# A linear recurrence computed ahead of 14 projection tiles, with another form of its factor, over eight banks

## The chip, the core and the metric

One core of a Trainium2 chip runs the whole program in a single launch. The metric is the device time of one execution in microseconds (us); all arithmetic is in float32.

## What is computed

The reference is a transformer layer followed by a second layer of another kind, for one sequence of 256 positions of width 1024. The first layer is a feed-forward block, a mixer and a second feed-forward block. The change lies in the mixer. Cut to what matters:

```python
proj = u @ w_in[l]                                   # 8704 columns
q, k, v, xr, yr, gl = jnp.split(proj, splits, axis=-1)
...                                                  # attention -> attn_d
xc = conv(xr) + conv_b                               # causal, width 4, per channel
gate_x = sigmoid(einsum(xc, w_x) + b_x)
gate_a = sigmoid(einsum(xc, w_a) + b_a)
log_a = -8.0 * gate_a * softplus(-a_param)
a = exp(log_a)
b = sqrt(-expm1(2.0 * log_a)) * (gate_x * xc)
h[t] = a[t] * h[t-1] + b[t]                          # over the 256 positions
rec_d = (h * gelu(yr)) @ w_rec_branch[l]
gates = sigmoid(gl)                                  # two sets of 1024
merged = gates[0] * attn_d + gates[1] * rec_d
h_out = h_in + rms_norm(merged @ w_out[l], mix_norm_post[l])
```

The second layer adds modulation from a condition vector, a grid shift, a bidirectional recurrent mixer with a Fourier part, and a feed-forward of 32 experts of which each position uses 4.

## The kernel before, in words

Activations of the mixer stand with channels on the 128 partitions and the 256 positions along the free dimension; a tile is 128 channels by 256 positions and is one accumulation in one of PSUM's eight banks (`ps[:, bank, 0:S]`). Weights come through a ring of eight slots of 128x3072 floats in SBUF. SP sends one load after the other in a fixed order (`send`, L389); load n waits until slot n-8 has been used (`w_used`). `N_WIN`, `N_LRU`, `N_ATT`, `N_REC`, `N_OUT` are the places in that order: 23 slots of `w_in` (three tiles each, the last two), two of the recurrence gates, two of the attention branch, three of the recurrence branch, three of the output projection. Then come 22 slots of the second feed-forward, with 16 of the modulation in between.

Each engine's program is written out by hand, and engines meet by semaphores; `up(name)` counts an event, `at(name, n)` awaits its n-th, `now(name)` the last one so far. Several events share a semaphore (`SHARED`, L190), so their order there is that of the engine's program.

After q, k, v and the attention, the mixer's rest runs as follows.

- TensorE (`rec_pe`, L722): 32 tiles of eight matmuls each over four banks (`proj_pe`, L520, matmul L529): 8 tiles of xr, 8 of yr, 16 of the gates gl. A tile waits until the one four before it has been read. Then 16 tiles of the recurrence gates with two matmuls each over eight banks (L746), the attention branch (8 tiles of four matmuls, L529), the recurrence branch (8 tiles of eight, L529), and the output projection (`out_pe`, L773, matmul L782), which waits until all eight merged tiles are there. From the fifth tile on, the attention branch waits until VectorE has merged the tile four before it.
- ScalarE (`rec_act`, L879): gelu on the yr tiles (L886), sigmoid on the gl tiles (L888), sigmoid on the recurrence gates (L892), eight tanh of -log_a (L897), one exp of log_a over all 128x2048 (L899), one square root over the same size (L902). A change of function table is an instruction of its own, ACT_TABLE_LOAD. Then the norm behind the output projection: two sums of squares (L414) and a small square root (L417).
- VectorE (`rec_dve`, L791): the convolution (five operations a tile, L824 to L832), gate_x times xc (L838), log_a (L843), then the factor under the root from t = tanh(-log_a), since 1 - a^2 = 2t / (1 + t): t + 1 (L847), reciprocal (L849), times t (L851), each over 128x2048. Then the attention branch's eight merges (L855), the product under the recurrence (L858), eight scans (L861), times gelu(yr) (L863), and the recurrence branch's merges (L867, L869).

Much later, the expert stage begins with the experts 0 and 1; `bias_up_pe` (L2125) adds their biases by a matmul whose weights are columns of the computed order `perm`. Its call is in `moe_pe`.

Of the kernel before, what the change touches and what calls it, by code (L numbers as in the profile page):

```python
# [14 lines left out]
P = 128  # L15
D = 1024
KD = D // P
S = 256
# [33 lines left out]
N_LRU = N_WIN + 23  # L52
N_ATT = N_LRU + 2
# [8 lines left out]
assert N_MOE % RING == 0  # L62

# [33 lines left out]
def shape_constants():  # L97
# [42 lines left out]
    cols["expert"] = np.tile(e, 4)[:, None]  # L140
    cols["room"] = np.tile(BS - np.array(CAPACITY)[None], (P, 1))
# [36 lines left out]
for _name, _rows in COLUMN_ROWS:  # L178
    if _n // P != (_n + _rows - 1) // P:
# [11 lines left out]
    "pe_1": (("cols_tp", 1), ("ext_mm", 12), ("qk", 16), ("v", 4), ("att_scores", 8), ("rec", 21), ("lru", 14),  # L191
# [3 lines left out]
    "act_1": (("sp_exp", 1), ("qk_out0", 12), ("v_out0", 4), ("att_exp", 8), ("gate_out", 24), ("lru_gate", 16),  # L195
              ("lru_tanh", 8), ("lru_sqrt", 1), ("cs", 2), ("p_read", 20), ("lora", 2), ("xcs", 8), ("spec", 4),
              ("fno", 4), ("catT", 2), ("rowb", 4), ("ek", 2)),
    "dve_1": (("cols", 2), ("ext", 12), ("qk_out1", 12), ("v_out1", 4), ("att_scored", 8), ("decay8", 1),
              ("xr_out", 8), ("lru_gx", 8), ("lru_ratio", 1), ("att_merged", 8), ("recT", 1), ("rec_merged", 8),
# [15 lines left out]
def build(nc, x, out):  # L215

    with ExitStack() as ctx:
# [144 lines left out]
        for i in range(23):  # L362
            wide(N_WIN + i, x["w_in"][0], 384 * i, min(384, 8704 - 384 * i), KD)
# [156 lines left out]
        def proj_pe(pe, tag, n, tiles, i0, freed, kt=KD, src=None, width=S, lo=0):  # L520


            landed(pe, n)
            src = uT if src is None else src
            w = slot(n)[:, 0:kt * tiles * P].rearrange("p (k n) -> p k n", k=kt)
            for c in range(tiles):
                freed(i0 + c)
                for k in range(kt):
                    ins = pe.matmul(ps[:, (i0 + c) % 4, 0:width], w[:, k, c * P:(c + 1) * P], src[:, k, lo:lo + width],  # L529
                                        start=(k == 0), stop=(k == kt - 1))  # L530
                ins.then_inc(*up("w_used" if c == tiles - 1 else tag))
# [18 lines left out]
        REC = tiles_of(N_WIN + 12, (3,) * 10 + (2,))  # L550
# [171 lines left out]
        def rec_pe(pe):  # L722
# [8 lines left out]
            for s in range(11):  # L731
                proj_pe(pe, "rec", N_WIN + 12 + s, 3 if s < 10 else 2, 3 * s, freed)

            pe.wait_ge(*at("xc", LH))
            for gi in range(2):
                n = N_LRU + gi
                landed(pe, n)
                w = slot(n)[:, 0:2048].rearrange("p (q k n) -> p q k n", q=4, k=2)
                for o in range(LH):
                    i = gi * LH + o  # L740
                    if i < 4:
                        pe.wait_ge(*at("gate_out", 24 - 3 + i))
                    elif i >= 8:
                        pe.wait_ge(*at("lru_gate", i - 7))
                    for k in range(2):
                        ins = pe.matmul(ps[:, i % 8, 0:S], w[:, o // 2, k, (o % 2) * P:(o % 2 + 1) * P], xc[:, o // 2 * 2 + k, :],  # L746
                                            start=(k == 0), stop=(k == 1))
                    ins.then_inc(*up("w_used" if o == LH - 1 else "lru"))

            i = 0  # L750
            for n, tiles in ((N_ATT, 6), (N_ATT + 1, 2)):
                def freed(i):
                    if i < 4:
                        pe.wait_ge(*at("lru_gate", 8 + i + 1))
                    else:
                        pe.wait_ge(*at("att_merged", i - 3))
                proj_pe(pe, "attb", n, tiles, i, freed, kt=4, src=attnT)
# [3 lines left out]
            for n, tiles in ((N_REC, 3), (N_REC + 1, 3), (N_REC + 2, 2)):  # L761
# [5 lines left out]
                proj_pe(pe, "recb", n, tiles, i, freed, src=lb)  # L767
                i += tiles

            pe.wait_ge(*at("rec_merged", LH))  # L770
            out_pe(pe, N_OUT, merged)

        def out_pe(pe, n0, src):  # L773

            for k in range(KD):
                n = n0 + k // 3
                if k % 3 == 0:
# [13 lines left out]
        def rec_dve(d):  # L791
# [72 lines left out]
            d.wait_ge(*now("recT"))  # L864
            for t in RECB:
                tile_done(d, "recb", t)
                d.tensor_tensor(gates[:, 8 + t[1], :], ps[:, t[1] % 4, 0:S], gates[:, 8 + t[1], :], ALU.mult).then_inc(*up("dve_own"))  # L867
# [11 lines left out]
        def rec_act(a):  # L879
# [9 lines left out]
            for t in LRU_G:  # L889
                tile_done(a, "lru", t)  # L890
                dst = lb if t[1] < LH else la
                a.activation(dst[:, t[1] % LH, :], ps[:, t[1] % 8, 0:S], ACT.Sigmoid,  # L892
# [1285 lines left out]
        def moe_pe(pe, turns):  # L2178
# [8 lines left out]
            def first(s):  # L2187
# [6 lines left out]
                bias_up_pe(pe, [perm[:, r:r + 1] for r in BLOCKS[s]])  # L2194
# [320 lines left out]
```

## Time and profile before

| what | value |
|---|---|
| median of 3 runs | 2480.01 us (2478.4 to 2480.95) |
| profiled execution, own time | 2474.24 us |
| its span | 2472.4 us |
| granted TensorE clock, mean | 0.957 |
| TensorE busy | 2228.3 us (90%) |
| VectorE busy | 763.5 us (31%) |
| ScalarE busy | 305.7 us (12%) |
| HBM traffic | 234 GB/s over the span |

The span runs from the first to the last instruction that the profiler saw; the own time is that of the same execution from outside. Starts are counted from the span's beginning. PE is TensorE's matmuls, PEld its weight loads, DVE VectorE, ACT ScalarE, POOL GpSimd, SP the engine that issues the weight loads. A float32 matmul of the program appears as two records. The granted clock is a share of 2.4 GHz.

### The profile page before, as it was taken

The page shows a single profiled execution, that of the slowest core. Times are in us where ns is not written, and L with a number is a line of the kernel's source. Part 1 is how long each engine was busy: PE and PEld are TensorE (multiplying, and loading weights), DVE is VectorE, ACT ScalarE, POOL GpSimd, SP SyncE. Part 2 cuts the span into 40 slices and gives each one's busy share as a digit, 9 for nine tenths or more (in the row PEclk, how much of TensorE's full clock was granted, in tenths as well). Part 3 has the DMA queues.
Part 4 walks back from the last instruction along what each step waited for, and adds up shares of the span by engine and source line. Part 5 has one row for each costly group of instructions (what it writes and reads, how often), then busy time and mean ns, then how long its engine had stood idle before and what let it go on. Part 6 is the DMA issues. An engine that isn't in the chain of part 4 may idle for free.

```text
span 2472.4 us, 34348 instructions
## 1 busy us (share of the span) xinstructions
PE 2228.3 (90%) x15028; PEld 1372.9 (56%) x15029; DVE 763.5 (31%) x1257; ACT 305.7 (12%) x563; POOL 102.3 (4%) x117
## 2 busy tenths in 40 slices
PE   7999798996799994989998759999999999999995
PEld 5667685885477763467777634444344344334431
DVE  1000102405265407346778451121121121211123
ACT  1000101012100000243433200000000000000000
POOL 0000000000100000211221100000000000000000
PEclk9999999997999996999999969999999999999998
DMA  9555443242668960000000347999999999999995
GB/s 315 175 161 172 136 152 102 94 136 94 199 218 280 284 194 15 1 3 3 3 3 3 134 182 311 414 419 417 417 416 416 417 414 416 416 416 416 414 417 203
DMA packets 232599, 581.07 MB, mean 235 GB/s; under 512 B 10341, under 2 KB 154497, under 8 KB 199553
## 3 DMA queue, kind: packets, MB, share of 16 engines
q1 hardware_dynamic: 227472, 562.07, 60.0%
q0 software_dynamic: 4560, 14.83, 1.7%
q8 instruction: 120, 1.97, 0.3%
q10 hardware_dynamic: 416, 1.94, 0.2%
q14 instruction: 31, 0.25, 0.0%
HBM read 575.40 MB, written 3.41 MB: 234 GB/s over the span
## 4 chain that ended last, share of the span: by engine, by line
PE 79%; DVE 9%; DMA 4%; SPq 3%; ACT 2%; issue 1%; POOL 0%; DVEq 0%; ACTq 0%; POOLq 0%
PE ps L2138 18%; PE ps L461 13%; PE ps L529 9%; PE ps L2150 7%; PE ps L470 6%; PE ps L1015 4%; DMA ring<-in_w 4%; SPq L2064 3%; PE ps L2162 3%; PE ps L782 2%; PE ps L2117 2%; PE ps L613 2%; PE ps L1356 2%; PE ps L1376 1%; PE ps L1373 1%
## 5 line engine op out<-in xcount | busy, mean ns | idle before, releaser
L2138 PE MATMUL ps<-ring,arena 128*64 128x512 f32 (+1 forms) x2048 | 502.7, 595 | 11.7 <-DMA ring<-in_w 11.7
L2138 PEld LDWEIGHTS ps<-ring,arena 128*64 128x64 f32 (+1 forms) x2048 | 178.1, 144 | 335.1 <-issue 335.0
L461 PE MATMUL ps<-arena,ring 128*128 128x256 f32 x1408 | 315.3, 383 | 1.7 <-DVE arena L440 1.7
L461 PEld LDWEIGHTS ps<-arena,ring 128*128 128x128 f32 x1408 | 266.4, 191 | 49.5 <-issue 12.3
L2150 PE MATMUL ps<-ring,arena 128*64 128x512 f32 (+1 forms) x1024 | 253.8, 594 | 16.4 <-DMA ring<-in_w 16.4
L529 PE MATMUL ps<-arena,ring 128*128 128x256 f32 x1088 | 240.9, 385 | 25.7 <-DVE arena L855 13.2
L529 PEld LDWEIGHTS ps<-arena,ring 128*128 128x128 f32 x1088 | 209.8, 193 | 56.3 <-DVE arena L855 13.6
L2150 PEld LDWEIGHTS ps<-ring,arena 128*64 128x64 f32 (+1 forms) x1024 | 88.8, 143 | 169.3 <-issue 167.8
L2320 DVE TENSOR_SCALAR arena<-ps 128x1024 f32<-128x1024 f32 x18 | 22.0, 1225 | 487.9 <-PE ps L2138 487.9
L470 PE MATMUL ps<-ring,arena 128*128 128x512 f32 x352 | 157.9, 592 | 0.0
L1015 PE MATMUL ps<-arena,ring 128*128 128x256 f32 (+1 forms) x320 | 106.4, 497 | 4.6 <-DVE arena L1080 4.6
L470 PEld LDWEIGHTS ps<-ring,arena 128*128 128x128 f32 x352 | 66.9, 190 | 66.3 <-issue 64.1
L2331 DVE COPY arena<-ps 128x1024 f32<-128x1024 f32 x18 | 22.1, 1225 | 249.3 <-PE ps L2157 249.3
L1015 PEld LDWEIGHTS ps<-arena,ring 128*128 128x128 f32 x320 | 62.8, 197 | 48.2 <-issue 38.3
L977 DVE SCALAR_TENSOR_TENSOR arena<-ring,arena 128x384 f32<-128x384 f32 x154 | 88.3, 615 | 2.5
L499 DVE TENSOR_TENSOR arena<-arena,ps 128x256 f32<-128x256 f32 x44 | 18.4, 418 | 221.8 <-ACT arena L491 221.8
L2271 ACT ACTIVATE arena<-ps 128x256 f32<-128x256 f32 x18 | 6.9, 384 | 581.6 <-PE ps L2122 581.6
L491 ACT ACTIVATE arena<-ps 128x256 f32<-128x256 f32 x44 | 16.9, 384 | 463.4 <-PE ps L461 463.4
L2162 PE MATMUL ps<-arena 128*128 128x512 f32 x144 | 66.6, 605 | 3.6 <-ACT arena L2289 2.1
L2117 PE MATMUL ps<-arena 128*128 128x128 f32 x576 | 68.9, 279 | 0.0
L2117 PEld LDWEIGHTS ps<-arena 128*128 128x128 f32 x576 | 67.4, 196 | 0.0
L2335 DVE TENSOR_TENSOR arena<-arena,ps 128x1024 f32<-128x1024 f32 x36 | 44.0, 1222 | 43.9 <-PE ps L2162 43.9
(435 smaller groups left out, 2153.5 us busy)
## 6 DMA issues: line engine op xcount, KB each, us to landing
ring<-in_w SPq DMA_DIRECT2D x384, 1024.0 KB, 16.9
ring<-in_w_in SPq DMA_DIRECT2D x26, 1536.0 KB, 6.8
ring<-in_w_ada SPq DMA_DIRECT2D x16, 1536.0 KB, 9.3
ring<-in_ffn_w_gate SPq DMA_DIRECT2D x44, 512.0 KB, 4.1
ring<-in_ffn_w_up SPq DMA_DIRECT2D x44, 512.0 KB, 5.4
ring<-in_ffn_w_down SPq DMA_DIRECT2D x44, 512.0 KB, 6.5
ring<-in_w_out SPq DMA_DIRECT2D x4, 1536.0 KB, 8.8
ring<-in_w_in SPq DMA_DIRECT2D x5, 1024.0 KB, 5.1
```

Source lines behind the costliest of these rows:

```text
L461: ins = pe.matmul(ps[:, j % 2, half * S:(half + 1) * S], s[:, col0:col0 + P], uT[:, k, :], start=(k == 0), stop=(k == KD - 1))
L470: ins = pe.matmul(ps[:, 4 + 2 * tt + nh, :], hid[:, j % 3, tt * P:(tt + 1) * P], s[:, 2048 + nh * 512:2048 + (nh + 1) * 512], start=(j == ...
L529: ins = pe.matmul(ps[:, (i0 + c) % 4, 0:width], w[:, k, c * P:(c + 1) * P], src[:, k, lo:lo + width], start=(k == 0), stop=(k == kt - 1))
L613: ins = pe.matmul(ps[:, i % 4, 0:384], uT[:, k, tt * P:(tt + 1) * P], w[:, k, :], start=(k == 0), stop=(k == KD - 1))
L782: ins = pe.matmul(ps[:, 4 + 2 * tt + nh, :], src[:, k, tt * P:(tt + 1) * P], w[:, nh * 512:(nh + 1) * 512], start=(k == 0), stop=(k == KD ...
L977: d.scalar_tensor_tensor(o, w[:, k, :], cs[:, k, m:m + 1], o, ALU.mult, ALU.add).then_inc(*up(f"ada_sum{m}"))
L1015: ins = pe.matmul(ps[:, i % 4, lo:2 * S], w[:, k, c * P:(c + 1) * P], hT2[:, k, lo:2 * S], start=(k == 0), stop=(k == KD - 1))
L2064: e.dma_start(chunk(n).rearrange("p (j n) -> p j n", j=2), x["w2_2"][0, expert, 2 * c * P:2 * (c + 1) * P, :].rearrange("a (j p) n -> p (a ...
L2117: ins = pe.matmul(banks(6, 2)[:, k * BS:(k + 1) * BS], h2[:, tt, k * P:(k + 1) * P], sel[:, tt, :], start=(tt == 0), stop=(tt == 1))
L2138: ins = pe.matmul(ps[a * n:(a + 1) * n, q, :], xsT[:, k, a * n:(a + 1) * n], chunk(at_ + a)[:, q * 512:(q + 1) * 512], start=False, stop=( ...
L2150: ins = pe.matmul(ps[a * n:(a + 1) * n, 4 + nh, :], actT[:, 2 * c + j, a * n:(a + 1) * n], chunk(at_ + a)[:, lo:lo + 512], start=(c == 0 a ...
L2162: ins = pe.matmul(ps[:, 4 + 2 * tt + nh, :], src[:, tt * P:(tt + 1) * P], ys[:, nh * 512:(nh + 1) * 512], start=True, stop=True)
```

## The change

The 32 projection tiles are cut into 18 (xr, yr and the first two tiles of gl; the slots of `w_in` after the 18th, `REC_BEFORE`, hold the other 14) and 14. The recurrence gates' two slots and their tiles come between them, in SP's order and in TensorE's. ScalarE does gates, tanh, eight exp of 2 log_a, exp and square root before the sigmoids of the 14 tiles (`gate_out2`); VectorE does the recurrence whole before the attention branch's merges. The factor is (1 + a^2) t, which is the same as 1 - a^2: eight operations of one tile each, without a reciprocal. The gates' and the 14 tiles go round eight banks (`lru_bank`), the two branches round four of them in another order (`branch_bank`). The output projection waits tile by tile. The first expert block takes the columns of its order from a constant, `own`, instead of from `perm`.

```diff
-N_LRU = N_WIN + 23
-N_ATT = N_LRU + 2
+REC_BEFORE = 18
+N_LRU = N_WIN + REC_BEFORE
+N_ATT = N_WIN + 23 + 2
...
+def win_slot(i):
+    return N_WIN + i + (2 if i >= REC_BEFORE else 0)
...
+    cols["own"] = (np.arange(P) % NE)[:, None] == np.arange(2)[None]
...
-        REC = tiles_of(N_WIN + 12, (3,) * 10 + (2,))
+        REC = tiles_of(N_WIN + 12, (3,) * 6)
+        REC2 = tiles_of(win_slot(REC_BEFORE), (3,) * 4 + (2,))
+        NREC = len(REC)
+
+        def lru_bank(i):
+            return (4 + i) % 8
+
+        def branch_bank(i):
+            return (2 + i) % 4
...
-            for s in range(11):
-                proj_pe(pe, "rec", N_WIN + 12 + s, 3 if s < 10 else 2, 3 * s, freed)
+            for s in range(6):
+                proj_pe(pe, "rec", N_WIN + 12 + s, 3, 3 * s, freed)
...
-                    if i < 4:
-                        pe.wait_ge(*at("gate_out", 24 - 3 + i))
-                    elif i >= 8:
+                    if i >= 8:
                         pe.wait_ge(*at("lru_gate", i - 7))
+                    elif i >= 4:
+                        pe.wait_ge(*at("gate_out", NREC - LH))
...
+            def freed(i):
+                if i < 8:
+                    pe.wait_ge(*at("lru_gate", i + 9))
+                else:
+                    pe.wait_ge(*at("gate_out2", i - 7))
+            for s in range(5):
+                proj_pe(pe, "rec2", win_slot(REC_BEFORE + s), 3 if s < 4 else 2, 3 * s, freed, bank=lru_bank)
...
-                    if i < 4:
-                        pe.wait_ge(*at("lru_gate", 8 + i + 1))
+                    if i < 2:
+                        pe.wait_ge(*at("gate_out2", i + 7))
+                    elif i < 4:
+                        pe.wait_ge(*at("gate_out2", i + 11))
                     else:
                         pe.wait_ge(*at("att_merged", i - 3))
...
-            pe.wait_ge(*at("rec_merged", LH))
-            out_pe(pe, N_OUT, merged)
+            out_pe(pe, N_OUT, merged, lambda k: pe.wait_ge(*at("rec_merged", k + 1)))
...
-            d.wait_ge(*at("lru_tanh", LH))
-            d.tensor_scalar_add(xc[:, :, :], lb[:, :, :], 1.0).then_inc(*up("dve_own"))
-            d.wait_ge(*now("dve_own"))
-            d.reciprocal(xc[:, :, :], xc[:, :, :]).then_inc(*up("dve_own"))
-            d.wait_ge(*now("dve_own"))
-            d.tensor_tensor(xc[:, :, :], xc[:, :, :], lb[:, :, :], ALU.mult).then_inc(*up("lru_ratio"))
-            d.wait_ge(*now("lru_ratio"))
-            for t in ATTB:
-                tile_done(d, "attb", t)
-                d.tensor_tensor(merged[:, t[1], :], ps[:, t[1] % 4, 0:S], gates[:, t[1], :], ALU.mult).then_inc(*up("att_merged"))
-                d.wait_ge(*now("att_merged"))
+            for j in range(LH):
+                d.wait_ge(*at("lru_square", j + 1))
+                d.scalar_tensor_tensor(xc[:, j, :], xc[:, j, :], 1.0, lb[:, j, :], ALU.add, ALU.mult).then_inc(*up("lru_ratio"))
             d.wait_ge(*at("lru_sqrt", 1))
...
             d.tensor_tensor(lb[:, :, :], lb[:, :, :], yg[:, :, :], ALU.mult).then_inc(*up("recT"))
-            d.wait_ge(*now("recT"))
+            for t in ATTB:
+                tile_done(d, "attb", t)
+                d.tensor_tensor(merged[:, t[1], :], ps[:, branch_bank(t[1]), 0:S], gates[:, t[1], :], ALU.mult).then_inc(*up("att_merged"))
+                d.wait_ge(*now("att_merged"))
...
                 a.activation(lb[:, j, :], la[:, j, :], ACT.Tanh, scale=-1.0).then_inc(*up("lru_tanh"))
-            a.wait_ge(*at("lru_tanh", LH))
+            for j in range(LH):
+                a.activation(xc[:, j, :], la[:, j, :], ACT.Exp, scale=2.0).then_inc(*up("lru_square"))
+            a.wait_ge(*now("lru_square"))
             a.activation(la[:, :, :], la[:, :, :], ACT.Exp).then_inc(*up("act_own"))
-            a.wait_ge(*now("act_own"))
-            a.wait_ge(*at("lru_ratio", 1))
-            a.activation(xc[:, :, :], xc[:, :, :], ACT.Sqrt, scale=2.0).then_inc(*up("lru_sqrt"))
+            a.wait_ge(*at("lru_ratio", LH))
+            a.activation(xc[:, :, :], xc[:, :, :], ACT.Sqrt).then_inc(*up("lru_sqrt"))
+            for t in REC2:
+                tile_done(a, "rec2", t)
+                a.activation(gates[:, NREC - 2 * LH + t[1], :], ps[:, lru_bank(t[1]), 0:S], ACT.Sigmoid).then_inc(*up("gate_out2"))
...
-                bias_up_pe(pe, [perm[:, r:r + 1] for r in BLOCKS[s]])
+                bias_up_pe(pe, [perm[:, r:r + 1] if s else k_("own", r, 1) for r in BLOCKS[s]])
```

## Rows read from the trace of the kernel before

**Rows 1.** The page: busy time of each engine, and TensorE's granted clock in 40 slices.

```profile
PE 2228.3 (90%) x15028; PEld 1372.9 (56%) x15029; DVE 763.5 (31%) x1257; ACT 305.7 (12%) x563; POOL 102.3 (4%) x117
...
PEclk9999999997999996999999969999999999999998
```

**Rows 2.** Timeline of TensorE, 439 to 680 us: start, duration, what, [idle before <- releaser].

```profile
439.32 110.77 PE L529 MATMUL ps<-arena,ring 128*128 128x256 f32 x512 [0.52 <-DVE arena L701]
549.93 13.98 PE L746 MATMUL ps<-arena,ring 128*128 128x256 f32 x64
563.74 7.07 PE L529 MATMUL ps<-arena,ring 128*128 128x256 f32 x32
584.02 9.68 PE L529 MATMUL ps<-arena,ring 128*128 128x256 f32 x32 [13.21 <-DVE arena L855]
604.73 30.28 PE L529 MATMUL ps<-arena,ring 128*128 128x256 f32 x128 [11.04 <-DVE arena L863]
636.06 27.73 PE L782 MATMUL ps<-ring,arena 128*128 128x512 f32 x64 [1.05 <-DVE arena L869]
676.46 3.68 PE L449 MATMUL ps<-const,arena 128*128 128x128 f32 x16 [12.66 <-DVE arena L435]
```

**Rows 3.** Timeline of VectorE, 566 to 605 us.

```profile
566.97 1.23 DVE L847 TENSOR_SCALAR arena<-arena 128x2048 f32<-128x2048 f32 x1 [2.09 <-ACT arena L897]
568.23 12.95 DVE L849 RECIPROCAL arena<-arena 128x2048 f32<-128x2048 f32 x1
581.22 2.29 DVE L851 TENSOR_TENSOR arena<-arena 128x2048 f32<-128x2048 f32 x1
583.54 1.80 DVE L855 TENSOR_TENSOR arena<-ps,arena 128x256 f32<-128x256 f32 x4
...
596.59 5.77 DVE L861 TENSOR_TENSOR_SCAN arena<-arena 128x256 f32<-128x256 f32 x8
602.39 2.29 DVE L863 TENSOR_TENSOR arena<-arena 128x2048 f32<-128x2048 f32 x1
```

**Rows 4.** Stretches: busy by engine, granted clock, DMA share, GB/s (the last three).

```profile
680.99:925.30 244.31, 244.29 (x1012) 183.15 (x1012) 104.22 (x198) 8.45 (x22) 0.71 (x1) 0.99 0.76 243
580.00:585.00 5.00, 0.98 (x2) 0.83 (x3) 4.83 (x6) 1.40 (x2) 0.00 (x0) 0.50 0.00 0
605.00:610.00 5.00, 5.00 (x13) 3.99 (x14) 0.00 (x0) 0.00 (x0) 0.00 (x0) 0.54 0.00 0
...
439.32:549.90 110.58, 110.58 (x512) 97.38 (x513) 22.79 (x68) 11.40 (x25) 0.00 (x0) 1.00 0.35 114
1766.00:2440.00 674.00, 649.96 (x2920) 267.25 (x2916) 125.93 (x171) 43.99 (x50) 0.00 (x0) 1.00 1.01 415
```

**Rows 5.** Timeline of ScalarE, 564 to 570 us.

```profile
564.32 2.55 ACT L897 ACTIVATE arena<-arena 128x256 f32<-128x256 f32 x8
566.88 1.28 ACT L899 ACT_TABLE_LOAD   x1
568.17 1.91 ACT L899 ACTIVATE arena<-arena 128x2048 f32<-128x2048 f32 x1
```

**Rows 6.** Groups by line and shape, 430 to 680 us: busy, mean ns.

```profile
L888 ACT ACTIVATE arena<-ps 128x256 f32<-128x256 f32 x16 | 6.1, 384 | 47.8 <-PE ps L529 47.8
...
L832 DVE SCALAR_TENSOR_TENSOR arena<-arena,cols 128x256 f32<-128x256 f32 x8 | 3.9, 485 | 0.3
```

**Rows 7.** Timeline of ScalarE around three other places.

```profile
495.28 1.28 ACT L888 ACT_TABLE_LOAD   x1
...
666.46 0.20 ACT L417 ACTIVATE stat<-stat 128x2 f32<-128x2 f32 x1 [0.37 <-DVE stat L422]
...
927.86 1.28 ACT L417 ACT_TABLE_LOAD   x1 [0.28 <-DVE stat L422]
```

**Rows 8.** Waits of SP, 430 to 700 us: total us, times, longest.

```profile
SPq L398 <- PE ps L529: 207.8, 16, 48.8
```

**Rows 9.** DMA issues, 430 to 680 us: KB each, median us to landing.

```profile
ring<-in_w_rec_branch SPq DMA_DIRECT2D x2, 1536.0 KB, 6.9
```

More of the change, by code:

```diff
@@ L190 @@
 SHARED = {
-    "pe_1": (("cols_tp", 1), ("ext_mm", 12), ("qk", 16), ("v", 4), ("att_scores", 8), ("rec", 21), ("lru", 14),
+    "pe_1": (("cols_tp", 1), ("ext_mm", 12), ("qk", 16), ("v", 4), ("att_scores", 8), ("rec", 12), ("lru", 14), ("rec2", 9),
              ("attb", 6), ("recb", 5), ("hT2_tp", 8), ("in2", 12), ("xcs_mm", 8), ("spec_mm", 4), ("fno_mm", 4),
@@ L362, in build @@
         for i in range(23):
-            wide(N_WIN + i, x["w_in"][0], 384 * i, min(384, 8704 - 384 * i), KD)
+            wide(win_slot(i), x["w_in"][0], 384 * i, min(384, 8704 - 384 * i), KD)
         for i, name in enumerate(("lru_w_x", "lru_w_a")):
@@ L518, in build, with proj_pe @@
         SCALE = 1.0 / math.sqrt(P)
-        def proj_pe(pe, tag, n, tiles, i0, freed, kt=KD, src=None, width=S, lo=0):
+        def proj_pe(pe, tag, n, tiles, i0, freed, kt=KD, src=None, width=S, lo=0, bank=lambda i: i % 4):
             landed(pe, n)
@@ L528, in proj_pe @@
                 for k in range(kt):
-                    ins = pe.matmul(ps[:, (i0 + c) % 4, 0:width], w[:, k, c * P:(c + 1) * P], src[:, k, lo:lo + width],
+                    ins = pe.matmul(ps[:, bank(i0 + c), 0:width], w[:, k, c * P:(c + 1) * P], src[:, k, lo:lo + width],
                                         start=(k == 0), stop=(k == kt - 1))
@@ L752, in freed @@
                 def freed(i):
-                    if i < 4:
-                        pe.wait_ge(*at("lru_gate", 8 + i + 1))
+                    if i < 2:
+                        pe.wait_ge(*at("gate_out2", i + 7))
+                    elif i < 4:
+                        pe.wait_ge(*at("gate_out2", i + 11))
                     else:
                         pe.wait_ge(*at("att_merged", i - 3))
-                proj_pe(pe, "attb", n, tiles, i, freed, kt=4, src=attnT)
+                proj_pe(pe, "attb", n, tiles, i, freed, kt=4, src=attnT, bank=branch_bank)
                 i += tiles
@@ L766, in freed, with out_pe @@
                         pe.wait_ge(*at("rec_merged", i - 3))
-                proj_pe(pe, "recb", n, tiles, i, freed, src=lb)
+                proj_pe(pe, "recb", n, tiles, i, freed, src=lb, bank=branch_bank)
                 i += tiles
-            pe.wait_ge(*at("rec_merged", LH))
-            out_pe(pe, N_OUT, merged)
-        def out_pe(pe, n0, src):
+            out_pe(pe, N_OUT, merged, lambda k: pe.wait_ge(*at("rec_merged", k + 1)))
+        def out_pe(pe, n0, src, ready=lambda k: None):
             for k in range(KD):
                 n = n0 + k // 3
+                ready(k)
                 if k % 3 == 0:
@@ L863, in rec_dve @@
             d.tensor_tensor(lb[:, :, :], lb[:, :, :], yg[:, :, :], ALU.mult).then_inc(*up("recT"))
-            d.wait_ge(*now("recT"))
+            for t in ATTB:
+                tile_done(d, "attb", t)
+                d.tensor_tensor(merged[:, t[1], :], ps[:, branch_bank(t[1]), 0:S], gates[:, t[1], :], ALU.mult).then_inc(*up("att_merged"))
+                d.wait_ge(*now("att_merged"))
             for t in RECB:
                 tile_done(d, "recb", t)
-                d.tensor_tensor(gates[:, 8 + t[1], :], ps[:, t[1] % 4, 0:S], gates[:, 8 + t[1], :], ALU.mult).then_inc(*up("dve_own"))
+                d.tensor_tensor(gates[:, 8 + t[1], :], ps[:, branch_bank(t[1]), 0:S], gates[:, 8 + t[1], :], ALU.mult).then_inc(*up("dve_own"))
                 d.wait_ge(*now("dve_own"))
@@ L891, in rec_act @@
                 dst = lb if t[1] < LH else la
-                a.activation(dst[:, t[1] % LH, :], ps[:, t[1] % 8, 0:S], ACT.Sigmoid,
+                a.activation(dst[:, t[1] % LH, :], ps[:, lru_bank(t[1]), 0:S], ACT.Sigmoid,
                                         bias=col("lru_b_x" if t[1] < LH else "lru_b_a", t[1] % LH)).then_inc(*up("lru_gate"))
```

8 lines of the change are left out of this document (4 added, 4 removed).

## The prediction

> **What bounds the kernel now.** I read the page first: TensorE is busy 90% of the span, VectorE 31%, ScalarE 12%, and the slices of the granted clock are at 9 tenths in 36 of 40, but the tenth of them, from 556 to 618 us, is at 7 [rows 1]. TensorE is the bound, so the question is where it stands still or runs slowly. The timeline of TensorE from 439 us, where this part of the mixer begins, answers it [rows 2]: 32 projection tiles without a gap (512 records, 110.77 us, 3.46 us a tile), the 16 tiles of the two recurrence gates (13.98), four attention-branch tiles (7.07), then nothing for 13.21 us; four more (9.68 instead of 7.07), nothing for 11.04; the eight recurrence-branch tiles in 30.28; nothing for 1.05; the output projection, 27.73. VectorE's timeline tells what was awaited [rows 3]: one reciprocal over 128x2048 takes 12.95 us, with 1.23 and 2.29 around it, and the merges of the attention branch, queued behind it, are what frees TensorE's four banks. After them come a product of 2.29 over the same size as the one shown, eight scans (5.77) and the last product (2.29), on which the recurrence branch waits. The clock by stretches [rows 4] gives the second half of the price: in 580 to 585 us it is granted at 0.50, that is 1.2 of 2.4 GHz, after ten us of idleness, and again about 0.54 in 605 to 610, after the second idle stretch; in the unbroken 439 to 550 it is 1.00.
>
> **The change on TensorE.** The work is the same: 18 + 14 = 32 projection tiles, 16 gate tiles, 8, 8, and the output. Only the order differs: 14 tiles that need nothing of the recurrence stand behind the recurrence gates, 14 x 3.46 = 48.4 us of cover. If all of it is enough, these terms go [rows 2]: idle 13.21 + 11.04; slow clock 9.68 - 7.07 = 2.61 in the attention branch; 30.28 - 110.77/4 = 2.59 in the recurrence branch (its 128 records are a quarter of the 512); and 1.05 at the output projection, whose first seven k steps now ask only for the merge of their own tile, while the eighth comes some 24 us later. Sum 30.5 us. Laid end to end: 439.3 + 110.8 + 13.8 + 13.8 + 27.7 + 27.7 = 633.1 against an end at 663.8, 30.7; I take 30.5.
>
> **Is the cover enough?** The gates end at 563.9 now, so at 515.4 with 14 tiles fewer before them. ScalarE [rows 5]: tanh 0.4 + 2.55, to 518.4; a table load 1.28; eight squares by exp, priced as the eight tanh, 2.6, to 522.3; exp over 128x2048, 1.91, to 524.3. VectorE makes the factor a tile behind the squares, 8 x 0.49 by the convolution's three-operand rows [rows 6], from 520.1 to 524.1. Table load and square root, priced as the exp of the same size, 3.2: 527.5. Product, scans, product 10.4: 537.9, the recurrence ready. ScalarE loads the sigmoid table (1.28) and begins on the 14 moved tiles at 528.8, three of them waiting; at 0.38 a tile [rows 6] against 3.46 on TensorE it catches up in four or so.
> - First wait: of the moved tiles, the ninth needs the first one's bank. TensorE is there at 515.4 + 8 x 3.46 = 543.1; the bank is free at 529.2. Margin 14 us.
> - Second: the fifth attention tile (570.7) needs the first merge, now queued on VectorE behind the recurrence, ready at 537.9 and then only a tile behind. Margin 32 us, and 39 for the recurrence branch (577.6).
> - The gates' tiles 5 to 8 need the last of the 18 projections read: it ends at 501.6, is read by 502.1, and TensorE is at the fifth gate at 505.1. The convolution works on the first eight of the 18, at five operations of up to 0.49 us a tile [rows 6] against 3.46. Nothing.
>
> So the new form of the factor is worth nothing by itself here: it saves about 12.6 us on VectorE (12.95 + 1.23 + 2.29 against 3.9) and costs ScalarE 2.6, both inside the margin; kept, the reciprocal would put the root's end at 538.1, the first bank at 539.8 against 543.1, and the recurrence at 548.5 against 570.7. If the cover were gone it would be worth those 12.6. Eight banks: with four, the fifth moved tile (529.2) would need the bank that is free at 529.2, so they are worth 0 to 3 us. Here a rule can be weighed. Rows: the 32 tiles run over four banks with no idle at all [rows 2]. The Trainium skill (Perfetto Trace Analysis, "Matmuls") has independent groups rotate through different PSUM banks so that evacuation overlaps; by it alone one would hope for a gain in every tile, but where TensorE has no idle time between tiles there is none to gain.
>
> **What is added on the path.** ScalarE's last table used to be the square root's, and the norm behind the output projection begins with a square root: it starts 0.37 us after its wait, with no load [rows 7]. The same line at 927.86 us, where the engine comes from another function, first loads 1.28 us, after the wait [rows 7]. Now the 14 sigmoids come last, so the first kind becomes the second: VectorE's reciprocal and all that follows are 1.28 us late, with TensorE idle anyway. The bounds are 0 (the load placed ahead of the wait, as the sigmoid's at 495.28 was [rows 7]) and 1.28; the same line is the nearest row, so 1.28. The other added load is in the chain above. The Trainium skill (ScalarE: Activation LUTs, "Table sets: the hidden batching unit") speaks against this order: calls should be batched by table set, and a load is put at about 2.7 us. By that figure the net would be an estimated 27.8 us instead of 29.2; the row's 1.28 decides.
>
> **Queues.** SP sends the same loads, the two gate blocks five places earlier; it waits for a free slot, not for bytes: all its waits from 430 to 700 us are for TensorE, 21 in number, the 16 longest in total shown [rows 8], and TensorE waits for no load there. Behind the output projection the second feed-forward draws 243 GB/s where 415 was moved later [rows 4]. GpSimd has no instruction in the stretch that moves. The constant table is two columns wider, and the first expert block reads its order from there rather than from the computed one; it still waits for the accumulators, so 0. All later starts (weights, experts) hang on semaphores of this chain and shift with it.
>
> Sum: -30.5 + 1.3 = -29.2. Profiled execution: span 2472.4 to 2443.2, own time 2474.24 to 2445.0. That execution is 5.8 under the median of the runs shown; against the median, 2480.01 - 29.2 = 2450.8.
>
> **Rivals.**
> - A wait in the place of the old one: TensorE stalls at the ninth moved tile or the fifth attention tile. The chain must be 14 us longer than laid out above. For: ScalarE's operations are in strict order, and everything hangs on the root. Against: every duration has its row. At 24 us longer it costs 10, and 2461. Chance 0.04.
> - Loads: the ring of eight slots is drained faster, and the second feed-forward starts with slots missing. For: 30 us less of quiet DMA. Against: [rows 8], and each slot is asked for seven slots ahead, over 50 us, while 1.5 MB land in 6.9 [rows 9]. One slot missing is about 7 us: 2458. Chance 0.05.
> - Given back later: the expert stage moves 415 GB/s at a full DMA share; if its transfers and not this chain set the end, the gain vanishes: 2480. Against: it starts on semaphores of the chain that now ends earlier, and its ring is full or empty by them alone. Chance 0.03.
> - Slower: the granted clock falls in the now unbroken stretch from 501.6 to 633. It decides once more than 29 us of work runs at 1.2 GHz; if all 131 us did, 2582; if 50 us did, 2501. Against: 244 us of the second feed-forward at 0.99 and 110 us over four banks at 1.00 [rows 4]. The Trainium skill (TensorE: Matmul & The Clock Gate, "A second HAM failure mode: psum-queue depth-cycling") tells of a kernel that cycled through banks and whose clock swung between its two levels because of the small pauses. By that rule the eight banks would lose time here; the trace disagrees as far as it goes. Chance 0.03.
> - The change doesn't do what it says: half of the idle time had another cause than VectorE's queue. Excluded by [rows 3], whose ends meet TensorE's starts within 0.1 us. Chance 0.01, 2465.
>
> **Numbers.** Forecast 0.84, 2450.8. What a measurement of this kernel can tell from no change is about 0.2%, 5 us. Range: from a gain of 31 (load hidden, four banks' worth gained) with 5 us for where the median falls and how the clock ramps meet the shifted starts, 2444, to 2459, which takes in the loads rival. Faster 0.94, same 0.03, slower 0.03.
>
> **What would show it.** TensorE from 439 to 633 us without an idle piece over 1 us and its clock at 1.00; the gates' matmuls near 502; the root's end near 527.5, the recurrence near 538; a table load of 1.28 us between the output projection and the square root of its norm; the next transposes at 676.5 - 29.2 = 647.3. It is wrong if TensorE idles in the moved tiles (first rival), if the later stages don't shift by the same 29 us (second, third), or if the clock is under 1.00 before 633 (fourth).

## The result, and the profile after

| | before | after |
|---|---|---|
| median of the runs | 2479.67 us (4 runs, 2478.4 to 2480.95) | 2444.86 us (4 runs, 2443.57 to 2449.59) |
| profiled execution, own time | 2474.24 us | 2449.59 us |
| its span | 2472.4 us | 2447.5 us |

The ratio is 0.9863, with a 95% interval of 0.9846 to 0.988: 34.8 us less, where 29.2 were forecast. The two profiled executions alone give 24.7 us. Both are explained below; first the stretch that was changed. From the page of the changed kernel, answering to [rows 1]:

```profile
PE 2228.5 (91%) x15028; PEld 1376.9 (56%) x15029; DVE 750.1 (31%) x1262; ACT 310.8 (13%) x573; POOL 102.4 (4%) x117
...
PEclk9999899999899987999999959999999999999998
```

The tenth slice of the clock, 551 to 612 us, is at 9 where it was at 7; the eleventh, at 8, holds the pause behind the output projection, which is still there. TensorE's timeline, answering to [rows 2]:

```profile
443.42 62.43 PE L535 MATMUL ps<-arena,ring 128*128 128x256 f32 x288 [0.52 <-DVE arena L715]
505.68 13.98 PE L760 MATMUL ps<-arena,ring 128*128 128x256 f32 x64
519.49 89.95 PE L535 MATMUL ps<-arena,ring 128*128 128x256 f32 x416
609.28 27.63 PE L806 MATMUL ps<-ring,arena 128*128 128x512 f32 x64
650.86 3.67 PE L455 MATMUL ps<-const,arena 128*128 128x128 f32 x16 [13.95 <-DVE arena L441]
```

The 18 tiles, the 16 gate tiles, then one unbroken run of the 14 moved tiles and both branches (416 records, 89.95 us), then the output projection without a pause. From the first projection tile to the output projection's end it is 609.28 + 27.63 - 443.42 = 193.49 us; before it was 636.06 + 27.73 - 439.32 = 224.47 [rows 2]. The granted clock of the stretch, answering to [rows 4] (the last three numbers are the clock, the DMA share and GB/s):

```profile
443.50:637.00 193.50, 193.41 (x832) 157.91 (x832) 52.03 (x125) 31.76 (x64) 0.00 (x0) 1.00 0.46 150
```

ScalarE and VectorE do the recurrence meanwhile. ScalarE's timeline, answering to [rows 5]:

```profile
520.07 2.54 ACT L916 ACTIVATE arena<-arena 128x256 f32<-128x256 f32 x8
522.63 1.28 ACT L918 ACT_TABLE_LOAD   x1
523.92 2.56 ACT L918 ACTIVATE arena<-arena 128x256 f32<-128x256 f32 x8
526.51 1.91 ACT L920 ACTIVATE arena<-arena 128x2048 f32<-128x2048 f32 x1
528.44 1.28 ACT L922 ACT_TABLE_LOAD   x1
529.74 1.91 ACT L922 ACTIVATE arena<-arena 128x2048 f32<-128x2048 f32 x1
531.67 1.28 ACT L925 ACT_TABLE_LOAD   x1
532.96 1.21 ACT L925 ACTIVATE arena<-ps 128x256 f32<-128x256 f32 x4
```

VectorE's, answering to [rows 3]:

```profile
524.45 2.78 DVE L872 SCALAR_TENSOR_TENSOR arena<-arena 128x256 f32<-128x256 f32 x8 [3.82 <-ACT arena L918]
531.68 2.29 DVE L874 TENSOR_TENSOR arena<-arena 128x2048 f32<-128x2048 f32 x1 [4.46 <-ACT arena L922]
534.01 5.77 DVE L877 TENSOR_TENSOR_SCAN arena<-arena 128x256 f32<-128x256 f32 x8
539.81 2.29 DVE L879 TENSOR_TENSOR arena<-arena 128x2048 f32<-128x2048 f32 x1
569.77 0.42 DVE L882 TENSOR_TENSOR arena<-ps,arena 128x256 f32<-128x256 f32 x1 [27.67 <-PE ps L535]
```

The gates' matmuls end at 519.5. The root is there at 531.65, the recurrence at 542.10, 22.6 us behind the gates; VectorE then idles until the first attention tile, at 569.77. Behind the output projection stands the new table load, answering to [rows 7]:

```profile
639.56 1.28 ACT L423 ACT_TABLE_LOAD   x1 [0.35 <-DVE stat L428]
640.85 0.20 ACT L423 ACTIVATE stat<-stat 128x2 f32<-128x2 f32 x1
```

It starts 0.35 us after VectorE's sum and puts the root 1.28 us later; the next transposes start 13.95 us behind the output projection in place of 12.67.

### The profile page after: what moved, and what is told of

Its sections match the earlier page's. It is cut to its first block, busy times and chain, and to the rows that moved or that the text cites. A ratio compares the mean times of both kernels' runs of the same rounds, so it can differ in the third digit from the quotient of the medians.

```text
span 2447.5 us, 34362 instructions
## 1 busy us (share of the span) xinstructions
PE 2228.5 (91%) x15028; PEld 1376.9 (56%) x15029; DVE 750.1 (31%) x1262; ACT 310.8 (13%) x573; POOL 102.4 (4%) x117
## 4 chain that ended last, share of the span: by engine, by line
PE 81%; DVE 8%; DMA 4%; SPq 3%; ACT 2%; issue 1%; POOL 0%; DVEq 0%; ACTq 0%; POOLq 0%
PE ps L2161 18%; PE ps L467 13%; PE ps L535 10%; PE ps L2173 8%; PE ps L476 6%; PE ps L1038 4%; DMA ring<-in_w 4%; SPq L2087 3%; PE ps L2185 3%; PE ps L806 2%; PE ps L2140 2%; PE ps L627 2%; PE ps L1379 2%; PE ps L1399 1%; PE ps L1396 1%
## 5 line engine op out<-in xcount | busy, mean ns | idle before, releaser
L535 PEld LDWEIGHTS ps<-arena,ring 128*128 128x128 f32 x1088 | 208.0, 191 | 30.5 <-DVE arena L446 1.3
```

Source lines behind the costliest of these rows:

```text
L535: ins = pe.matmul(ps[:, bank(i0 + c), 0:width], w[:, k, c * P:(c + 1) * P], src[:, k, lo:lo + width], start=(k == 0), stop=(k == kt - 1))
```

## The experiments

"Stretch" is the time from the first projection tile's start to the output projection's end on TensorE.

**The change once more, unedited.**

> The changed kernel once more, unedited, to learn how much of the difference between 29.2 us forecast and 34.8 us measured in the medians is chance. Theory (the gain is 31.0 us of TensorE idle and slow time less one table load of 1.28 us, and the rest is how the clock's ramps after pauses elsewhere happen to fall in each execution): against the kernel before 28 to 32 us in this round, ratio 0.987 to 0.989; in the profile the stretch from the first of the 18 tiles to the end of the output projection takes 193.5 us and from there to the next transposes 13.95, both within 0.3, whatever the whole time is. Rival (something behind the mixer also became faster): the ratio stays at 0.986 or below and a later stage is some 5 us shorter in every execution.

Measured: 2447.04 us (5 runs), the kernel before beside it 2480.05 (10 runs), ratio 0.9866, interval 0.9844 to 0.9889. That is 33.0 us, one more than the theory's 28 to 32, and the ratio is just under its lower end of 0.987. The stretch is 193.49 us and the pause 13.95, as expected. So what exceeds 29.7 is not in the mixer, and it is not this one set of runs either; see the repeats of the kernel before.

**The reordering with the old factor.**

```diff
-            for j in range(LH):
-                d.wait_ge(*at("lru_square", j + 1))
-                d.scalar_tensor_tensor(xc[:, j, :], xc[:, j, :], 1.0, lb[:, j, :], ALU.add, ALU.mult).then_inc(*up("lru_ratio"))
+            d.wait_ge(*at("lru_tanh", LH))
+            d.tensor_scalar_add(xc[:, :, :], lb[:, :, :], 1.0).then_inc(*up("dve_own"))
+            d.wait_ge(*now("dve_own"))
+            d.reciprocal(xc[:, :, :], xc[:, :, :]).then_inc(*up("dve_own"))
+            d.wait_ge(*now("dve_own"))
+            d.tensor_tensor(xc[:, :, :], xc[:, :, :], lb[:, :, :], ALU.mult).then_inc(*up("lru_ratio"))
...
-            for j in range(LH):
-                a.activation(xc[:, j, :], la[:, j, :], ACT.Exp, scale=2.0).then_inc(*up("lru_square"))
-            a.wait_ge(*now("lru_square"))
+            a.wait_ge(*at("lru_tanh", LH))
```

> The reordering kept, the factor by add, reciprocal and product again (VectorE 16.5 us in place of 2.8, ScalarE without the eight squares). Theory (the moved tiles cover it): TensorE stretch of 193.5 us as in the changed kernel, no idle piece over 1 us, time within 0.1% of the unedited change; the square root ends some 8 us later than with the new factor and the ninth moved tile still finds its bank free, with 3 us to spare. Rival (the factor matters beside the reordering): an idle piece at the ninth moved tile, time 3 us or more above the change.

Measured: 2448.08 us (4 runs), ratio to before 0.9873 (0.9847 to 0.99); the change, run beside it, 2447.04. ScalarE's timeline of this run:

```profile
524.20 1.28 ACT L923 ACT_TABLE_LOAD   x1
537.64 1.91 ACT L923 ACTIVATE arena<-arena 128x2048 f32<-128x2048 f32 x1 [12.15 <-DVE arena L875]
...
540.86 2.04 ACT L926 ACTIVATE arena<-ps 128x256 f32<-128x256 f32 x7
```

The root ends at 539.55, 21.7 us behind the gates (517.84, below) in place of 12.2, so 9.5 later where some 8 were expected; the first moved tiles are read from 540.86 on, and the ninth is reached at 545.5. TensorE's run of moved tiles and branches stays unbroken and as long:

```profile
517.84 89.95 PE L535 MATMUL ps<-arena,ring 128*128 128x256 f32 x416
```

With 14 tiles of cover the new factor is worth nothing that can be measured.

**The new factor without the reordering.** In the kernel before, the three operations over 128x2048 are replaced as in the diff of the change; the order of the tiles and the banks stay.

> The kernel before with the new factor alone: the 14 tiles are not moved, four banks. Theory: the first idle piece of TensorE shrinks from 13.2 to 1 or 2 us and the slow clock behind it goes (2.6 us), the second idle piece of 11 us stays with its slow clock; no table load is added. The recurrence branch starts at 590 in place of 604.7, and the time falls by 14 to 15 us, ratio 0.994. Rival (the reciprocal's time is covered by something else): the time falls by less than 5 us.

Measured: 2463.51 us (5 runs), ratio 0.9937 (0.9915 to 0.9959), 16.5 us less than before. TensorE's timeline of this run, the rows that answer to the fourth to sixth of [rows 2]:

```profile
574.45 7.17 PE L529 MATMUL ps<-arena,ring 128*128 128x256 f32 x32 [1.05 <-DVE arena L851]
592.67 29.27 PE L529 MATMUL ps<-arena,ring 128*128 128x256 f32 x128 [11.04 <-DVE arena L859]
622.99 27.73 PE L782 MATMUL ps<-ring,arena 128*128 128x512 f32 x64 [1.04 <-DVE arena L865]
```

The first idle piece is 1.05 us in place of 13.21 and the tiles behind it take 7.17 in place of 9.68; the second, 11.04, stays, and the matmuls behind it still run slowly, though less so than expected (29.27 in place of 30.28, against 27.7 at full clock). Stretch 208.81 us, 15.7 less than before; 14 to 15 were expected. So the two parts of the change overlap: alone, the factor saves 15.7 us of the stretch and the reordering 31.0; together they save 31.0.

**Four banks for the moved tiles.**

```diff
-                if i < 8:
+                if i < 4:
                     pe.wait_ge(*at("lru_gate", i + 9))
                 else:
-                    pe.wait_ge(*at("gate_out2", i - 7))
+                    pe.wait_ge(*at("gate_out2", i - 3))
...
-                proj_pe(pe, "rec2", win_slot(REC_BEFORE + s), 3 if s < 4 else 2, 3 * s, freed, bank=lru_bank)
+                proj_pe(pe, "rec2", win_slot(REC_BEFORE + s), 3 if s < 4 else 2, 3 * s, freed, bank=lambda i: 4 + i % 4)
...
-                a.activation(gates[:, NREC - 2 * LH + t[1], :], ps[:, lru_bank(t[1]), 0:S], ACT.Sigmoid).then_inc(*up("gate_out2"))
+                a.activation(gates[:, NREC - 2 * LH + t[1], :], ps[:, 4 + t[1] % 4, 0:S], ACT.Sigmoid).then_inc(*up("gate_out2"))
```

> The changed kernel with the 14 moved tiles on four banks (4 to 7) in place of eight. The fifth moved tile is reached 13.8 us behind the gates' last matmul; in the changed kernel's trace the first moved tile was read 13.9 us behind it. Theory (eight banks are worth next to nothing): one idle piece of 0.1 to 1 us at the fifth tile, stretch of 193.6 to 194.5 us. Rival by the rule that evacuation needs more banks: several idle pieces, 3 us or more.

Measured: one run, 2446.21 us. The run of moved tiles and branches is 0.20 us longer; stretch 193.69 us. The timeline shows it as one piece, but by its line's own waits TensorE was idle in it once, for 0.3 us, until ScalarE had read a moved tile; in the changed kernel that line has no idle time:

```profile
519.08 90.15 PE L535 MATMUL ps<-arena,ring 128*128 128x256 f32 x416
```

The eight banks are worth 0.2 us here, which is the coincidence of two numbers (13.8 us to the fifth tile, 13.9 to the first one's reading), and with a slower chain they would by the same reckoning be worth more, which no run shows.

**How much cover is needed: 5, 2, and 5 tiles with the old factor.** `REC_BEFORE` is 21 or 22 in place of 18, and the counts and waits follow.

> Only the last 5 of the 32 projection tiles behind the recurrence gates, not 14. In the changed kernel's trace the recurrence is ready 22.6 us behind the gates' last matmul and the first merge 0.5 us later; five tiles and the four attention tiles that need no merge are 17.3 + 6.9 = 24.2 us. Theory (the need for cover is 23 us, 14 tiles are far more than enough): no idle piece, stretch from the first projection tile to the output projection's end 193.5 us as with 14. Rival (more cover is needed than the chain shows): an idle piece at the fifth attention tile.

> Only the last 2 tiles moved: cover 6.9 + 6.9 = 13.8 us against a need of 23.1. Theory: one idle piece of 9.3 us at the fifth attention tile, released by VectorE's merge, then 1 to 3 us of matmuls at 1.2 GHz; stretch of 204 to 206 us. Rival: the idle piece is absent or over 12 us.

> Only 5 tiles moved, as in the run that had no idle piece, but with the old factor by reciprocal. With that factor and 14 tiles moved the recurrence was ready 32.2 us behind the gates' last matmul, 32.6 with the first merge; the cover is 24.2 us. Theory (the factor is worth its 10 us exactly when the cover is short): one idle piece of 8.4 us at the fifth attention tile and 1 to 3 us of slow clock behind it, stretch of 203 to 205 us. Rival: no idle piece, so something else than this chain sets the need.

Measured with five: one run, 2442.49 us, stretch 193.50, and one unbroken run behind the gates:

```profile
546.74 58.87 PE L535 MATMUL ps<-arena,ring 128*128 128x256 f32 x272
```

With two: 2459.10 us, stretch 204.17, an idle piece of 9.02 us released by VectorE's merge where 9.3 were expected:

```profile
559.75 13.98 PE L535 MATMUL ps<-arena,ring 128*128 128x256 f32 x64
582.74 36.20 PE L535 MATMUL ps<-arena,ring 128*128 128x256 f32 x160 [9.02 <-DVE arena L882]
```

With five and the reciprocal: 2455.18 us, stretch 203.66:

```profile
549.40 20.88 PE L535 MATMUL ps<-arena,ring 128*128 128x256 f32 x96
573.97 5.41 PE L535 MATMUL ps<-arena,ring 128*128 128x256 f32 x16 [3.68 <-ACT arena L926]
581.95 36.49 PE L535 MATMUL ps<-arena,ring 128*128 128x256 f32 x160 [2.58 <-DVE arena L885]
```

The wait is split, which had not been foreseen: 3.68 us for ScalarE, since the third attention tile needs the bank of the fifth moved tile, whose reading stands behind the root, and 2.58 us for VectorE's merge, 6.3 us in all where 8.4 were expected. The two tiles between ran largely at the slow clock (5.41 us for 16 records, against 7.07 for 32 in [rows 2]; granted 0.66 over 574 to 579 us), and TensorE began the fifth attention tile at 581.95, 32.6 us behind the gates (549.40), as the chain says. The need of cover is 23 us with the new factor and 33 with the old one; the reordering gives 55.

**The output projection waits for all tiles again.**

```diff
-            out_pe(pe, N_OUT, merged, lambda k: pe.wait_ge(*at("rec_merged", k + 1)))
+            pe.wait_ge(*at("rec_merged", LH))
+            out_pe(pe, N_OUT, merged)
```

> The changed kernel, but the output projection waits for all eight merged tiles again. Theory: one idle piece of 1.04 us before it, as in the kernel before, and nothing else; stretch from the first projection tile to the output projection's end 194.5 us instead of 193.5. Rival: no idle piece.

Measured: an idle piece of 1.04 us and a stretch of 194.80, 1.3 more than the change:

```profile
606.84 27.73 PE L807 MATMUL ps<-ring,arena 128*128 128x512 f32 x64 [1.04 <-DVE arena L889]
...
653.07 16.42 PE L467 MATMUL ps<-arena,ring 128*128 128x256 f32 x64 [0.85 <-DVE arena L446]
```

The whole time of this one run is 2452.51 us, 7.7 over the median of the change, where "nothing else" was expected. The second row shows a part of it: the second feed-forward's first 64 records took 16.42 us instead of 14.08. Another part lies in the second layer's recurrent mixer, a stretch that no edit touched, from the start of its first Fourier matmul to that of its output projection's last: 366.9 us here and 360.9 in the run with five moved tiles. The clock in the two, in this order, is 0.93 and 0.95:

```profile
1047.00:1414.00 367.00, 321.81 (x6896) 268.09 (x6896) 227.91 (x335) 126.67 (x253) 64.74 (x54) 0.93 0.11 41
```

```profile
1043.00:1404.00 361.00, 315.64 (x6895) 262.00 (x6896) 226.95 (x335) 126.66 (x254) 64.90 (x54) 0.95 0.11 40
```

**Without the constant.** The first expert block reads `perm` again, and the table loses its two columns.

> The changed kernel, but the first expert block reads the columns of the computed order again, and the constant table has its old width. Theory (this edit is worth nothing): from the first expert matmul to the end 976 to 978 us, as with the constant, and the pause before that block's bias 1.1 us as before. Rival: the pause or the stage differs by over 1 us.

Measured: one run, 2444.63 us; from the first expert matmul to the end 976.9 us, against 976.7 in the changed kernel, and the pause ahead of that block's bias is 1.11 us in both. The edit costs and brings nothing.

**The kernel before, twice more.**

> The kernel before once more, unedited, for a second profile: its profiled execution was 5.8 us under its median, and the medians differ by 34 us where the stretch and the table load give 29.7. Theory (the clock's ramps behind pauses vary from execution to execution): the stretch from the first projection tile to the output projection's end is 224 to 228 us, the two idle pieces are 13.2 and 11.0 as before to 0.1 us, and what differs in the whole time lies in matmuls at 1.2 GHz, here and behind other pauses. Rival: the idle pieces themselves are longer, or a stage with full clock is.

> A third profile of the kernel before. In the two so far the second feed-forward's first 64 matmul records took over 15.8 us, in every changed kernel 14.1, and the stage behind it 106.9 against mostly 105.6. Theory (chance of where the clock's ramp falls): at least one of the two is at the lower value this time. Rival (the moved pauses shift the ramps in a fixed way): both are at the upper values again.

Measured: 2479.83 and 2477.59 us. The two idle pieces are 13.21 and 11.04 us in both, and the stretches 224.74 and 224.45, against 224.47 in the first profile. From the timeline of the second one (TensorE; the third row is the second feed-forward's start):

```profile
586.69 9.86 PE L529 MATMUL ps<-arena,ring 128*128 128x256 f32 x32 [13.21 <-DVE arena L855]
607.58 30.37 PE L529 MATMUL ps<-arena,ring 128*128 128x256 f32 x128 [11.04 <-DVE arena L863]
...
683.95 15.93 PE L461 MATMUL ps<-arena,ring 128*128 128x256 f32 x64 [0.85 <-DVE arena L440]
```

The second layer's input projection:

```profile
971.93 106.38 PE L1015 MATMUL ps<-arena,ring 128*128 128x256 f32 x320 [4.62 <-DVE arena L1080]
```

The same two places in the changed kernel:

```profile
655.39 14.08 PE L467 MATMUL ps<-arena,ring 128*128 128x256 f32 x64 [0.85 <-DVE arena L446]
```

```profile
941.51 105.07 PE L1038 MATMUL ps<-arena,ring 128*128 128x256 f32 x320 [4.62 <-DVE arena L1103]
```

Both rows of before are at their longer value in all three profiles of the kernel before (15.89, 15.93, 15.89 and 106.36, 106.38, 106.36); in the eleven profiles of the changed kernel and its variants (the one with the factor alone among them) the first is longer once (16.42, above) and the second once (106.47, in the repeat of the change). The third run was meant to show at least one short value and did not. So chance alone is not the likely reading, but neither is a fixed shift shown: both lengths occur with the change. What differs is the granted clock: 0.88 over the first row in the first profile of before and 1.00 in the changed kernel, and over the first 11 us of the second 0.73 and 0.85 (0.72 in the repeat of the change, the one long case). What decides when it rises was not found. A third difference is at the end: from the last expert matmul of the first kind to the span's end it is 69.8 to 70.0 us in the three profiles of before, and 68.6 to 69.1 in the eleven others. The last two transfers land sooner (KB each, median us to landing; before, then after):

```profile
out<-arena SPq DMA_DIRECT2D x2, 512.0 KB, 3.1
```

```profile
out<-arena SPq DMA_DIRECT2D x2, 512.0 KB, 2.6
```

That accounts for some 0.5 us of it. No edit of the change touches them, and the kernel with the factor alone shows it too; its cause stays open.

**A version that beats both kernels.** It is the changed kernel with the root's table fetched early. The one-column square root below, whose result is not used, also stands behind the last silu of both feed-forwards, and the two silu of the condition columns are made right behind the recurrence.

```diff
                 a.activation(gates[:, NREC - 2 * LH + t[1], :], ps[:, lru_bank(t[1]), 0:S], ACT.Sigmoid).then_inc(*up("gate_out2"))
+            a.wait_ge(*at("recT", 1))
+            a.activation(cs[:, :, 0], col("c_2", 0, 8), ACT.Silu).then_inc(*up("cs"))
+            a.activation(cs[:, :, 1], col("c_ctx_2", 0, 8), ACT.Silu).then_inc(*up("cs"))
+            a.activation(stat[:, 63:64], k_("ident", 0, 1), ACT.Sqrt).then_inc(*up("act_own"))
+            a.wait_ge(*now("act_own"))
```

> The changed kernel, with ScalarE loading the square root's table while TensorE works: a one-column square root behind the last sigmoid of the moved tiles and behind the last silu of both feed-forwards, and the two silu of the condition columns made right behind the recurrence instead of between the two norms. Theory: the table loads of 1.28 us go from the path behind both feed-forwards and at both norms around the mixer's end, 4 x 1.28, and 0.3 for the silus: 5.4 us less than the change; from the output projection's end to the next transposes 11.1 us in place of 13.95. Rival (another wait ends last there): 13.95 falls by less than 2, the time by less than 3 us.

Measured: 2438.70 us (5 runs, 2434.34 to 2444.61), ratio to before 0.983 (0.9814 to 0.9846). ScalarE behind the first feed-forward loads the table while TensorE still works, 5 us ahead of the norm:

```profile
255.47 1.28 ACT L498 ACT_TABLE_LOAD   x1
256.76 0.20 ACT L498 ACTIVATE stat<-const 128x1 f32<-128x1 f32 x1
262.00 1.02 ACT L420 ACTIVATE arena<-ps 128x1024 f32<-128x1024 f32 x1 [5.03 <-PE ps L476]
```

At the mixer's end the root follows its wait without a load, and the next transposes start 645.31 - 634.04 = 11.27 us behind the output projection, not 13.95 (ScalarE, then TensorE):

```profile
636.76 0.20 ACT L423 ACTIVATE stat<-stat 128x2 f32<-128x2 f32 x1 [0.37 <-DVE stat L428]
```

```profile
645.31 3.43 PE L455 MATMUL ps<-const,arena 128*128 128x128 f32 x16 [11.28 <-DVE arena L441]
```

That is 2.68 us there. The pause behind the first feed-forward falls from 12.51 to 11.30 us, 1.2 less; from the output projection's start to the second layer's input projection it is 328.2 us in place of 332.2, so 1.3 more behind the second feed-forward. Together the trace shows 5.2 us of the 5.4 expected. The median, not measured beside the change's, is 8.3 us under that of its repeat and 6.2 under its first; with executions that spread over 10 us the surplus is not shown to be more than scatter.

## Why the prediction was right, and where it was short

**The terms on TensorE** were forecast at 30.5 us and are 224.47 - 193.49 = 31.0. All five went: both idle pieces, the two stretches at 1.2 GHz behind them, and the 1.05 us at the output projection, which the run that undid it brought back alone (1.04). End to end the forecast had 30.7. The half microsecond that the sum lacks is in the breaks themselves: rows that follow without a break overlap by 0.16 to 0.17 us (505.68 + 13.98 = 519.66 against 519.49), so each break costs that much beside its idle figure, and the output projection's row is 0.1 longer behind one (27.73 against 27.63). The run that brought back the 1.04 us lost 1.31.

**The cover** was right almost to the tenth. This execution came to the stretch 4.1 us later than the first profile of before, so 4.1 is to be taken off: the root's end at 531.65 - 4.1 = 527.5 (forecast 527.5), the recurrence at 538.0 (537.9). Inside the chain the factor took 0.35 us a tile and not 0.49, which counted for nothing: the exp and the table load ended later. The margin of 32 us at the fifth attention tile was tried from the other side: with nine tiles fewer there is no idle time, with twelve fewer 9 us.

**The factor and the eight banks** were put at nothing by themselves (the banks at 0 to 3 us), and the runs give 0.0 and 0.2 us of the stretch. What the forecast had wrong is the factor's worth without cover, "those 12.6". It left out the squares' 2.6 on ScalarE, though its own times for the root, 538.1 and 527.5, are only 10.6 apart; measured it is 9.5, since with the reciprocal the root's table was loaded early, while VectorE still worked. With five tiles moved, 24.2 us of cover against a need of 23.0, the two forms differ by 10.2 us: 8.3 for which the cover is short, and 1.9 of slow matmuls in the last row. In the old order the factor alone saves 15.7, of which 12.2 are idle time and 3.5 the slow clock behind it. It is the same idle time counted from its other end, and it shows that the parts do not add.

**The table load** was put at 1.28 us by the row of the same line in another place, and the pause grew by 13.95 - 12.67 = 1.28. The Trainium skill (ScalarE: Activation LUTs, "Table sets: the hidden batching unit") asks for calls to be batched by set, and this case agrees in that the split sigmoids cost a load on the path. Its price of about 2.7 us for a load is not what the rows show: every load here took 1.28, and the exp that ends at 526.51 + 1.91 = 528.42 is followed by the load at 528.44 and the root at 529.74, with no other cost in between. The last experiment kept the order and moved four loads off the path: the profile has 25 loads before, 27 after, and 26 there.

**The rivals** did not come in: no wait took the place of the old one, no load of weights was awaited, the gain was not given back, and the clock stayed at 1.00 through 193.5 us. What the Trainium skill tells of cycling through banks (TensorE: Matmul & The Clock Gate, "A second HAM failure mode: psum-queue depth-cycling") did not occur here: it speaks of small pauses between groups, and this run has none.

**What was mis-sized** is the last sentence on the queues, that all later starts shift with the chain, taken as a term of 0. By the traces the stages behind are not of constant length: in the changed kernel's first profile the second feed-forward's first matmuls are 1.8 us shorter than in any profile of before, the second layer's input projection 1.3 (not so in its repeat), the end 1.0 or more. The first two are the granted clock, as shown above; the causes stay open. The three and 31.0 - 1.28 make 33.8 us, against 34.8 and 33.0 in the two sets of medians. The forecast range, 2444 to 2459, held the median by 0.9 us, and owes that to the 5 us allowed for medians and clock ramps, not to its terms: what exceeds 29.7 was not foreseen, and that it stayed small was partly luck. And the sentence that set the profiled execution against the median was right to do so: with 2474.24 us it was a lucky one, 2.9 us shorter than the second profile up to the attention's values and 2.1 in the second layer's recurrent mixer; the changed kernel's profiled execution was the longest of its four, 3.8 us longer than its repeat up to the attention's values and 1.5 in that mixer. Against the first profile of before it was 4.1 us longer up to the stretch and 4.8 in that mixer, which is why the two alone show 24.7 us: 24.7 + 4.1 + 4.8 = 33.6. That mixer takes 359.3 to 361.4 us in the three profiles of before and 359.8 to 366.9 in the eleven others; whether that is scatter alone or partly the change's doing is not separated.

## What to carry to other kernels

Where two engines wait for each other around a serial chain, look for work that needs nothing of the chain, put it behind the chain's inputs, and work out the need of cover from the chain's rows: 23 us here, so 5 tiles would have done what 14 did. Parts of a change that attack the same idle time do not add up, so each is to be priced with the other in place. When an order of ScalarE's functions changes, follow its table to the next use on the critical path, where a load can appear in a place that no edit touches; a one-column call made early in idle time takes it off again.

## What the runs showed of the hardware that had not been expected

The kernel before ran in 2470.9 to 2486.2 us over ten executions, and in the three of its executions that were profiled the two idle pieces are equal to 0.01 us. The granted clock, as a mean over the span, goes with it: 0.959 in the fastest and 0.954 in the slowest. Those two were not profiled; in two variants of the changed kernel that were, such a difference lies in the second layer's recurrent mixer, 360.9 us at a clock of 0.95 and 366.9 at 0.93. And a table load stands ahead of the wait in one place and behind it in another: the root's in the run with the old factor was made at 524.20, 13 us before the root, while the kernel before made it after VectorE's factor, at 583.59. In the source the first has one wait ahead of the activation and the second has two in a row; that this is the reason was not tried. The other loads looked at fit it: in the changed kernel the norm's (639.56) and the silu's (644.04, after 2.98 us of waiting for VectorE) stand behind two waits in a row, and the moved sigmoids' (531.67), with one wait in the source, follows the root at once.
